# Two transformer blocks on one core: the first two products behind four norms interleaved over the tiles, the last square of four norms summed on TensorE, fewer activation table loads

## The reference

```python
def rms_norm(x, g):
    y = xf * lax.rsqrt(jnp.mean(xf * xf, axis=-1, keepdims=True) + EPS)
    return (y * g.astype(jnp.float32)).astype(x.dtype)
...
hx = modulate(rms_norm(x, g_pre_mix), sh_m, sc_m)           # norm 0 (norm 1: the same for ctx)
... project(hx, w_in) ...
x_new = x + gt_m * rms_norm(mix_x, g_post_mix)               # norm 2
hf = modulate(rms_norm(x_new, g_pre_ffn), sh_f, sc_f)        # norm 3
x_new = x_new + gt_f * rms_norm(swiglu(hf, ...), g_post_ffn) # norm 4
# second block: norm 5 ahead of hy_w_in, norm 6 ahead of ffn_w_up, norm 7 at the very end
```

## Time and profile before

| | |
|---|---|
| median of 3 runs | 1598.26 us (1598.25 to 1598.79) |
| the profiled execution | 1598.33 us, of which the span from first to last instruction is 1596.5 |
| TensorE busy | 1471.4 us (92%) |
| VectorE, ScalarE, GpSimd busy | 949.7, 520.7, 201.1 us |
| chain that ended last | 83% TensorE, 10% VectorE, 2% ScalarE, 2% GpSimd |
| mean granted clock of TensorE | 0.962 of full speed |

### The profile page before, as it was taken

The page is one execution under the profiler, slowest core; times in us unless marked ns, Lnnn a source line. Parts: engine busy times, 40 slices in busy tenths (PEclk is TensorE's granted clock), DMA queues, the critical chain, the costliest instruction groups (busy, mean ns, idle before and its releaser), DMA issues.

```text
span 1596.5 us, 17041 instructions
## 1 busy us (share of the span) xinstructions
PE 1471.4 (92%) x6184; PEld 1126.9 (71%) x6184; DVE 949.7 (59%) x1211; ACT 520.7 (33%) x732; POOL 201.1 (13%) x181
## 2 busy tenths in 40 slices
PE   8599999999969999999997899996597999999996
PEld 6488887455738888888872378863475888888884
DVE  6832477777256666662218746649835888887222
ACT  1423353444353223232223323220234333333221
POOL 4401530000200000000113200017311000000000
PEclk9999999999979999999997899997898999999998
DMA  7322230224307666662221032210021222323221
GB/s 267 118 86 73 93 99 21 79 79 164 112 18 257 206 227 215 214 233 95 91 82 63 0 117 94 92 40 0 1 92 60 99 93 91 105 92 127 91 72 53
DMA packets 45148, 168.06 MB, mean 105 GB/s; under 512 B 5579, under 2 KB 6155, under 8 KB 44140
## 3 DMA queue, kind: packets, MB, share of 16 engines
q1 hardware_dynamic: 43692, 164.55, 30.4%
q0 software_dynamic: 1408, 2.89, 0.7%
HBM read 162.44 MB, written 2.10 MB: 103 GB/s over the span
## 4 chain that ended last, share of the span: by engine, by line
PE 83%; DVE 10%; issue 2%; ACT 2%; POOL 2%; DMA 1%; SPq 0%; POOLq 0%; DVEq 0%; ACTq 0%
PE PS L564 67%; PE PS L838 3%; DVE tb L1624 2%; PE PS L938 2%; PE PS L801 1%; PE PS L800 1%; DVE H L1624 1%; PE PS L1024 1%; POOL acc L1526 1%; PE PS L593 1%; PE PS L611 1%; DMA wraw<-w_mod_a 1%; PE PS L621 1%; DVE zpD L2156 1%; DVE wsp L553 1%
## 5 line engine op out<-in xcount | busy, mean ns | idle before, releaser
L564 PE MATMUL PS<-H,wsp 128*128 128x512 f32 x3600 | 836.6, 394 | 29.2 <-DVE H L1624 18.0
L564 PEld LDWEIGHTS PS<-H,wsp 128*128 128x128 f32 x3600 | 680.4, 190 | 180.4 <-issue 18.8
L553 DVE TENSOR_TENSOR wsp<-wraw,wsp 128x1024 fp32r<-128x1024 f32 (+1 forms) x182 | 237.7, 1306 | 467.8 <-ACT wsp L547 467.7
L547 ACT ACTIVATE wsp<-wraw 128x1024 fp32r<-128x1024 f32 (+1 forms) x182 | 202.7, 1115 | 538.9 <-PE PS L564 537.0
L564 PE MATMUL PS<-hid,wsp 128*128 128x512 f32 x1056 | 239.7, 389 | 0.0
L564 PEld LDWEIGHTS PS<-hid,wsp 128*128 128x128 f32 x1056 | 198.2, 188 | 41.1
L1624 DVE SCALAR_TENSOR_TENSOR cva<-PS,dert,cva 128x441 f32<-128x441 f32 (+2 forms) x176 | 122.3, 695 | 5.5
L1523 POOL COPY acc<-sqb 128x512 f32<-128x512 f32 x5 | 5.1, 1014 | 766.6 <-ACT sqb L1346 282.5
L1526 POOL TENSOR_TENSOR acc<-acc,sqb 128x512 f32<-128x512 f32 x35 | 57.5, 1644 | 229.6 <-ACT sqb L1503 93.3
L1852 DVE CUSTOM_DVE_ANT_0 sink<-mring,crow_t,colt 128x1024 bf16<-128x1024 f32 x56 | 71.7, 1280 | 0.4
L1024 PE MATMUL PS<-invt,KS 128*128 128x256 f32 x128 | 32.2, 418 | 22.9 <-DVE row L2193 22.9
(11 more groups left out here) (276 smaller groups left out, 1449.7 us busy)
## 6 DMA issues: line engine op xcount, KB each, us to landing
mring<-mod_c SPq DMA_DIRECT2D x56, 512.0 KB, 4.5
wraw<-w_ffn_in SPq DMA_DIRECT2D x44, 512.0 KB, 3.3
wraw<-w_up SPq DMA_DIRECT2D x44, 512.0 KB, 3.3
wraw<-w_mod_b SPq DMA_DIRECT2D x24, 512.0 KB, 3.3
wraw<-w_hy_in SPq DMA_DIRECT2D x24, 512.0 KB, 3.3
wraw<-w_w_in SPq DMA_DIRECT2D x22, 512.0 KB, 3.3
wraw<-w_ffn_out SPq DMA_DIRECT2D x16, 704.0 KB, 4.1
wraw<-w_down SPq DMA_DIRECT2D x16, 704.0 KB, 4.0
```

Source lines behind the costliest of these rows:

```text
L547: nc.scalar.activation(wsp[:, o % 2, 0, 0:n], wraw[:, g % RAW, 0:n], ACT.Copy).then_inc(w_hi, 1)
L553: nc.vector.tensor_tensor(wsp[:, o % 2, 1, 0:n], wraw[:, g % RAW, 0:n], wsp[:, o % 2, 0, 0:n].bitcast(F32), ALU.subtract).then_inc(w_lo, 1)
L564: mm = nc.tensor.matmul(psum, wsp[:, o % 2, a, wk * P:(wk + 1) * P], h[:, b, kt, :], start=first and kt == kts[0] and (a, b) == (0, 0), st ...
```

## The change

1. At the four places behind norms the first two units are computed side by side: for each tile the three matmuls of the first unit, then the three of the second (`pair_matmuls`). `w_done` counts for both at the end. At `w_in` the latent part of both units comes first, then the context part of both.
2. VectorE computes the low parts of both units ahead of the norm's tiles, and ScalarE the high parts.
3. For norms 2, 4, 6 and 7, GpSimd adds seven squares only. TensorE adds the eighth (`sqb`) by a second matmul with the matrix of ones into the same PSUM bank.
4. `root` no longer loads the table set itself; `root_table` does it where Silu has displaced it: before `ffn_out`, before the units of `hy_out`, before `down`. Two loads fewer stand in the program.
5. On ScalarE, `split_hi` of `ffn_in` 0 and `hy_in` 0 stand behind `root` instead of ahead of it, `ffn_in` 1 stands among the squares of norm 3, and `up` 1 ahead of `root`.

```diff
+        LAST_ON_PE = (2, 4, 6, 7)
+        def acc_base(k):
+            return sum(KT - 1 if j in LAST_ON_PE else KT for j in range(k))
...
+        def pair_matmuls(pe, o, psums, h, ready):
+            last = []
+            for kt in range(KT):
+                pe.wait_ge(ready[0], ready[1] + kt + 1)
+                for u in range(2):
+                    for a, b in ((0, 0), (0, 1), (1, 0)):
+                        mm = nc.tensor.matmul(psums[u], wsp[:, (o + u) % 2, a, kt * P:(kt + 1) * P], h[:, b, kt, :],
+                                              start=kt == 0 and (a, b) == (0, 0),
+                                              stop=kt == KT - 1 and (a, b) == (1, 0))
+                    last.append(mm)
+            return last[-2:]
...
             def total(k):
-                pe.wait_ge(n_acc, KT * (k + 1))
+                pe.wait_ge(n_acc, acc_base(k + 1))
                 n = LC if k == 1 else L
-                nc.tensor.matmul(PS[:, 5 if k == 1 else 6, 0:n], ones[:, :], acc_of(k), start=True, stop=True).then_inc(n_ss, 1)
+                mm = nc.tensor.matmul(PS[:, 5 if k == 1 else 6, 0:n], ones[:, :], acc_of(k), start=True,
+                                      stop=k not in LAST_ON_PE)
+                if k in LAST_ON_PE:
+                    pe.wait_ge(n_sq, KT * (k + 1))
+                    mm = nc.tensor.matmul(PS[:, 6, :], ones[:, :], sqb[:, (KT - 1) % 2, :], start=False, stop=True)
+                mm.then_inc(n_ss, 1)
...
+            pe.wait_ge(w_lo, ORD["w_in"] + 2)
+            pair_matmuls(pe, ORD["w_in"], [PS[:, 0, :], PS[:, 1, :]], H, (n_h, 0))
+            for mm in pair_matmuls(pe, ORD["w_in"], [PS[:, 2, 0:LC], PS[:, 3, 0:LC]], Hc, (n_h, KT)):
+                mm.then_inc(w_done, 1)
+            aux(0)
...
                 def four(i, first):
-                    for u in range(4):
+                    if first:
+                        pe.wait_ge(w_lo, ORD[name] + 2)
+                        for mm in pair_matmuls(pe, ORD[name], [PS[:, 0, :], PS[:, 1, :]], H, (n_h, normed)):
+                            mm.then_inc(w_done, 1)
+                    for u in range(2 if first else 0, 4):
...
+            def root_table():
+                SC.preload_act_table_set("natural_log_exp_and_others")
             def root(k):
-                SC.preload_act_table_set("natural_log_exp_and_others")
...
-            split_hi(act, "ffn_in", 0)
             root(2)
+            split_hi(act, "ffn_in", 0)
             for kt in range(KT):
                 act.wait_ge(n_x, kt + 1)
                 square(3 * KT + kt, X[:, kt, :])
+                if kt == 2:
+                    split_hi(act, "ffn_in", 1)
             root(3)
-            split_hi(act, "ffn_in", 1)
...
             split_hi(act, "up", 0)
+            split_hi(act, "up", 1)
             root(6)
-            split_hi(act, "up", 1)
...
+            split_lo(dve, "w_in", 0)
+            split_lo(dve, "w_in", 1)
...
             scaled(0, X, "a_mix", (0, 1, 2, 3))
-            split_lo(dve, "w_in", 0)
             lows(0, 0, H, lambda kt: mod_col(0, kt), X, "a_mix")
             scaled(1, Xc, "a_ctx", (0, 1, 2, 3), LC)
-            split_lo(dve, "w_in", 1)
...
             residuals(2, Ym, "p_mix")
+            split_lo(dve, "ffn_in", 1)
             scaled(3, X, "a_ffn", (0, 1, 2, 3))
```

More of the change, by code:

```diff
@@ L905, in four @@
                             pe.wait_ge(free, i * 2 + (base + u // 2 - 1))
-                        split_matmuls(pe, ORD[name] + u, PS[:, u, :], H, range(KT), 0, True, True,
-                                      (n_h, normed) if first and u == 0 else None).then_inc(w_done, 1)
+                        split_matmuls(pe, ORD[name] + u, PS[:, u, :], H, range(KT), 0, True, True).then_inc(w_done, 1)
                 four(0, True)
@@ L986, in hy_four @@
             def hy_four(i, first):
-                for u in range(4):
-                    pe.wait_ge(w_lo, i * 4 + (ORD["hy_in"] + u + 1))
[L989 to L994, removed]
+                if first:
+                    pe.wait_ge(w_lo, ORD["hy_in"] + 2)
+                    pe.wait_ge(k_inv, 1)
+                    for mm in pair_matmuls(pe, ORD["hy_in"], [PS[:, 0, :], PS[:, 1, :]], H, (n_h, 3 * KT)):
+                        mm.then_inc(w_done, 1)
+                for u in range(2 if first else 0, 4):
+                    pe.wait_ge(w_lo, i * 4 + (ORD["hy_in"] + u + 1))
+                    pe.wait_ge(y_b, i * 4 + (u - 1))
+                    split_matmuls(pe, ORD["hy_in"] + u, PS[:, u % 2, :], H, range(KT), 0, True, True).then_inc(w_done, 1)
             hy_four(0, True)
@@ L1300, in _ @@
                 SC.activation(Ym[:, n, :], PS[:, n % 2, :], ACT.Copy).then_inc(n_y, 1)
+            root(2)
             split_hi(act, "ffn_in", 0)
-            root(2)
             for kt in range(KT):
@@ L1351, in _ @@
             down_four(3, True)
-            split_hi(act, "hy_in", 0)
             act.wait_ge(m_rd, MOD_B + MOD_C)
             root(4)
+            split_hi(act, "hy_in", 0)
             def squares(kts):
@@ L1437, in _ @@
             split_hi(act, "hy_out", 1)
+            root_table()
             for n in range(8):
@@ L1517, in sums @@
                 for kt in kts:
+                    if kt == KT - 1 and k in LAST_ON_PE:
+                        continue
                     q = k * KT + kt
@@ L2014, in _ @@
             residuals(2, Ym, "p_mix")
+            split_lo(dve, "ffn_in", 1)
             scaled(3, X, "a_ffn", (0, 1, 2, 3))
-            lows(3, 2 * KT, H, lambda kt: mod_col(3, kt), X, "a_ffn", range(0, 5))
-            split_lo(dve, "ffn_in", 1)
-            lows(3, 2 * KT, H, lambda kt: mod_col(3, kt), X, "a_ffn", range(5, KT))
+            lows(3, 2 * KT, H, lambda kt: mod_col(3, kt), X, "a_ffn")
             def ffn_four(i, first, last):
@@ L2227, in _ @@
             split_lo(dve, "up", 0)
+            split_lo(dve, "up", 1)
             scaled(6, X, "a_ffn2", (0, 1, 2, 3))
-            lows(6, 4 * KT, H, lambda kt: mod2_col(3, kt), X, "a_ffn2", range(0, 5))
-            split_lo(dve, "up", 1)
-            lows(6, 4 * KT, H, lambda kt: mod2_col(3, kt), X, "a_ffn2", range(5, KT))
+            lows(6, 4 * KT, H, lambda kt: mod2_col(3, kt), X, "a_ffn2")
             def up_low(i, j):
```

31 lines of the change are left out of this document (11 added, 20 removed).

## The result

| | before | changed |
|---|---|---|
| median | 1598.26 us (1596.06 to 1600.6, 15 runs) | 1601.78 us (1599.58 to 1604.21, 15 runs) |
| ratio | | 1.0021, 95% interval 1.0015 to 1.0028 |
| the profiled execution, span | 1598.33, 1596.5 us | 1604.21, 1602.4 us |
| mean granted clock | 0.962 | 0.960 |

The changed kernel is 3.5 us slower. That is little, but the interval excludes a ratio of 1. The forecast was 1599.0.

What follows compares the result with a forecast made beforehand. TensorE, busy 92% of the span, was taken as the bound, its first unit behind norms paced by VectorE's tiles. Terms -1.8, +0.6, 0, +1.8, +2.4, -2.3 summed to +0.7: 1599.0 us, range 1595.0 to 1603.0.

Steps and rivals of the forecast that it cites:

- `w_in`, -1.8: At `w_in`: low parts moved ahead and units paired, third unit starts at 92.5 instead of 94.29, 1.8 us gained.
- Norm 2 and `ffn_in`, +0.6: Norm 2 to `ffn_in`: high and low part delay `tb` by 0.7 us; third unit at 484.7 against 484.1, 0.6 lost.
- `hy_in`, +1.8: At `hy_in`: tiles are there long since, so pairing gains nothing, and the ring's stop adds 1.8 us.
- the first rival: Half-clock stretches follow the new stops: 1602.4 us with two, 1604.1 with three; slower, chance 0.22.
- Norm 6 and `up`, +2.4: At `up`: TensorE stops 2.5 us ahead of the third unit and 1.4 ahead of the fourth; 2.4 us lost, norm 6's 0.3 included.
- Norm 7, -2.3: At the end: one more matmul replaces sum and low adds, ending at 1583.1 instead of 1585.41, 2.3 us gained.
- The rival on half-clock stretches: Same as the first rival: four stops, at `w_in`, `ffn_in`, `hy_in` and `up`, may bring half clock; slower, chance 0.22.
- 2.2 for the clock: Behind norms 0, 3 and 6 a pair loses half of a 4.4 us half-clock stretch, 2.2 us at each place.
- the ring's stop: Behind a pair, the third unit's weights can be split only once the first unit is done; 1.81 us seen at `w_out`.
- norm 4, norm 6 and the table loads bring nothing: Norm 4: 0 taken; norm 6: +0.3 us; table loads: 0.1 at norm 3, the others 0, in ScalarE's waits.

Runs made afterwards that it cites:

- no_pairs_high_first: The changed kernel with units one by one at all four places and the high part of `ffn_in` 0 ahead of norm 2's Ln: 1589.57 us, ratio 0.9941.
- best_again: The same kernel as no_pairs_high_first, timed again beside the changed kernel: 1588.65 us, ratio 0.9932 to the kernel before.
- ffn_skewed: no_pairs_high_first with the first two units of `ffn_in` overlapped, the second three tiles behind the first: 1590.13 us, ratio 0.9936.

## Why the prediction was right, and what it misread

The time lay in the range, and 1.4 to 2.8 us above the forecast. By the prediction's own steps:

- **`w_in`, -1.8.** Right in kind: -1.14 to the first matmul. From there to the third unit it took 20.8 and 22.1 us in two traces, with 21.1 forecast. In the first the half-clock stretch of the pair was short (the clock rose 3.1 us behind the first matmul), in the second long (5.9). The reading that a pair pays half of this stretch and a single unit nothing holds: in seven traces with the pair the clock rose after 3.1 to 5.9 us, and the third unit came 20.8 to 22.1 us behind the first matmul, the later the rise the later; in the six with the low parts moved and no pair there the rise came after 3.1 to 5.1 us, and the third unit after 19.8 or 19.9.
- **Norm 2 and `ffn_in`, +0.6.** The high part and the low part stood in the way as forecast (`tb` 3.47 us behind Ln, 3.4 forecast). But from `w_out`'s end at 445.03 and 444.09 the first matmul came after 24.18 and 24.17 us: the 0.6 was given back between `tb` and norm 3's Ln, 13.92 us against 14.48. That was luck: the same stretch took 13.65 and 14.70 us in two traces of one and the same kernel (`no_pairs_high_first`, `best_again`). The stop of 1.81 was exact. From the first matmul to the third unit it is 14.6 instead of 14.9.
- **`hy_in`, +1.8.** The stop was exact, the stage cost 5.1. This is the term that was mis-sized, and the first rival is what was missing: 1.8 for the stop, 1.6 for the clock behind it, and some 1.4 since the clock at the start rose 5.9 us behind the first matmul instead of 3.0. I don't count that last part to the pair, since the late rise also stands in a trace without it (`ffn_skewed`: 160.1 us for the stage instead of 159.0); it is in four of the seven traces with the pair and one of the seven without. The clock fell behind this stop in three of the six traces that have it unfilled; the three others took 160.8 to 161.0 us, 2.0 more than unit by unit. The three in which it fell are just the three in which it had risen late at the start, so the stop's length alone doesn't decide; that is read from six traces and not tested. On average the pair cost about 2.8 there.
- **Norm 6 and `up`, +2.4.** Stops of 2.5 and 1.4 forecast, 2.40 and 1.12 found; the fourth unit 2.5 us later behind the first matmul. Later groups were to gain no further delay; the last product with `H` ends 2.9 us later behind the first matmul (247.7 against 244.8), so 0.4 was added.
- **Norm 7, -2.3.** 2.3 from the last product to Ln, 2.0 in the experiment.
- **The rival on half-clock stretches.** It had named four stops and told none of them from the others. It happened at `hy_in` alone. Behind the stops at `w_in`, `ffn_in` and `up`, in seven traces each, the clock never fell.

So the sums per place held to about 1 us, apart from `hy_in`, since they were made from measured starts of the third unit.

**What failed is the reading of where the gain comes from.** The prediction said that VectorE delivers a tile each 1.32 us and that the second unit of 5.44 us would vanish in the shadow of the first, less 2.2 for the clock. The last three tiles come 0.66 us apart. Alone, the first unit is done after 8.3 us, so TensorE waits only 8.3 - 5.4 = 2.9 us between tiles. Of that the half-clock stretch takes about 2 (free for a single unit, paid by a pair). What is left, 0.3 to 1.0 us, is less than the ring's stop of 1.8 that the pair brings. The pair loses at every place: 0.9 to 2.2 at `w_in`, 0.8 at `ffn_in`, 2.0 at `hy_in` (3.6 where the clock falls), 4.1 at `up`. That is 7.8 to 10.7 together, against 11.5 and 13 by the times; the late rise of the clock at `hy_in` may be part of the difference, and the rest is not placed.

What gained at `w_in`, `ffn_in` and `up` were the low parts that stood in the middle of the norm's tiles (1.1 us at `ffn_in`, 1.2 at `up`, at `w_in` 1.1 to the first matmul and 2.0 behind it) and have moved; the prediction booked these inside the pair's sum. The two together made the kernel look almost unchanged: some 6 us from the low parts and 2.0 from norm 7, taken back by the pairs, and 2 to 3.5 us more. That the forecast of the time came near doesn't bear out its reading of the pair: a gain and a loss that it had not told apart stood in one sum.

That norm 4, norm 6 and the table loads bring nothing was forecast and is not contradicted; they were not tried alone. Whether `ffn_skewed` is truly faster stays open: its 0.9 us is seen in the timeline and is below what these timings tell.

## What to carry to other kernels

Before interleaving two units to fill the waits between a producer's tiles, take from the trace when each tile comes, the last ones too, and compare what TensorE really waits (the unit alone, less its work) with what the end costs: two units that end together empty a double buffer, and the third then waits for the whole chain that refills it. If units must overlap, let the first run ahead and keep as much of the second behind as the refill takes; in the one trace of such an order no stop was left. And when a change has several parts, price each against the kernel with the other parts already in: here the simple move of four low and two high parts held most of the gain, and the elaborate part lost it.

## What was unexpected of the hardware

Stops of one and the same length are followed by a half-clock stretch in one execution and not in the next. Over the 14 traces of this study, the 1.81 us stop at `w_out` was followed by one in six, a wait of 1.26 us at about 248 us in four others, the 1.81 us stop at `hy_in` in three of six, and the stops of 1.8, 1.8, 2.4 and 1.1 us at `w_in`, `ffn_in` and `up` in none of seven. At `hy_in` the three with a stretch are those in which the clock had risen 5.8 to 6.0 us behind the first matmul, and the three without are those in which it had risen after 2.8 to 3.1. Two traces of the same kernel differ in this: the changed one has a stretch at 0.5 behind `w_out`'s stop in the first and none in the second, and that is 60.6 against 58.8 us to `ffn_in`. By the rule that the Trainium skill states ("TensorE: Matmul & The Clock Gate", "HAM oscillation"), only longer stops of TensorE bring the clock down. Here these short ones are followed by half clock, in some executions and not in others; at `hy_in` filling the stop kept the clock up. Each stretch costs about 1.6 to 1.8 us. A kernel with many such stops can't be priced to better than a few of these steps from one profile.
